# One decoder block kernel: head pairs issued in turn on TensorE, one score bank moved, search flags and the first residual rows reordered

## The chip, the cores and the metric

The kernel runs on one core of one Trainium2 chip, as one launch. The metric is the device time of a launch in microseconds (us). Three runs of the kernel before gave 3902.55, 3918.41 and 3919.11 us (median 3918.41). The profiled execution took 3900.74 us, of which its span is 3899.0 us.

## The reference

The input is x with 256 tokens of width 2048, float32. Two transformer blocks follow each other.

- Block one projects rms_norm(x) into four mixers: differential attention (4 heads, two 64-wide score maps a head), an RG-LRU, forgetting attention (4 heads of 128), and sliding-window attention with sinks (8 heads of 64, 2 key/value heads). Each is gated, the sum goes through w_out into the residual, and a SwiGLU feed-forward follows.
- Block two has dilated attention, NSA attention, cross attention to 256 memory rows, and a PEER layer.
- NSA has 16 query heads of 64 on 2 key/value heads. Each head attends in three branches: to 15 compressed keys, to the selected keys, and to a window. With 256 tokens the second and third use the same causal mask here. The three outputs are weighted by sigmoid gates and added.
- PEER has 8 heads. Each takes the 16 best of 128 by 128 expert pairs out of two sums of 128 scores, softmaxes them into gates, and all 16384 experts are computed densely: `gelu(v @ expert_u.T)` times the gate matrix, times `expert_v`.

What the change touches is, in the reference's words:

```python
logits = einsum('bqhmd,bshmd->bmhqs', q, k)     # differential, 2 maps of 64
logits = einsum('bnqkgd,bnskd->bnkgqs', q, k)   # sliding window, heads of 64
out    = einsum('bnkgqs,bnskd->bnqkgd', p, v)
# NSA: the same for compressed, selected and window keys, heads of 64
# PEER: top 16 of pair sums -> softmax -> dense gates; h += (gelu(x U) * gates) V
```

## The kernel before

Activations lie feature-major: 16 chunks of 128 features by 256 tokens. Every weight chunk is 1 MB (128 partitions by 2048 floats). SyncE's queue brings the chunks, in the order of `weight_stream`, into a ring of four. For float32 accuracy each chunk is split in two halves of 1024 columns. ScalarE writes the rounded part `wh` (L1130) and VectorE the remainder `wl` (L1768). Both hold four halves, so they can be at most two chunks ahead of TensorE. TensorE multiplies with three products: wh by x high and wh by x low (L519, L520), then wl by x high (L527). A chunk is one output tile (`tile_T`), 48 matmuls, and its result lies in PSUM bank 0 or 1 until ScalarE has evacuated it. A block of rows of a residual product (`rows`, L608, L610, L615) accumulates into all 8 banks instead.

No planner orders the work. Each engine's program is written out by hand, and they meet on counters: `full_a/full_v` says that a bank is ready for ScalarE or VectorE, `free_a/free_v` that it was read. `reserve(b)` lets TensorE wait for both free counters of a bank. `take(b)` is the reader's wait.

- **Pairs of heads.** Queries of two 64-wide heads (or two maps) lie in partitions 0 to 63 and 64 to 127 of one tile `qs`. The scores of a head are two float32 matmuls, for query block 0 against 128 keys and query block 1 against 256 (L682, helper `qk`). Differential and sliding-window attention call `qk` once per head. NSA calls it four times a pair, head by head and in a head branch by branch, into banks 2 to 5. A float32 matmul leaves two records in the trace.
- **Values.** `pv_T` (L701, L702) multiplies a head's probabilities for key block 0 (256 queries) and key block 1 (128 queries) with values of 64 columns. The heads of a pair write partitions 0 to 63 and 64 to 127 of bank 6. `nsa_values` does head 0 with two branches and its compressed product (L959, 15 rows), then head 1.
- **Order in an NSA pair.** Tile, transposed probabilities of the previous pair (L695, L948), tile, compressed scores into banks 6 and 7 (L975), scores, values of the previous pair, tile, tile (from pair 4 on a product `parts_T` in place of the last tile). VectorE reads the compressed scores at L2347, then the scores (L1859), takes the maximum, and normalises after ScalarE's exps. ScalarE evacuates the third tile's gate (L1514) only after its exps. From pair 4 on VectorE applies gates to banks 2 to 5 (L2387).
- **Search.** 128 expert tiles follow in PEER: 112 tiles, 64 rows of expert_v (`residual("v0")`), 16 tiles, 64 rows (`residual("v1")`). During the first 28 tiles VectorE also runs the top-16 searches, 8 parts a head. After every two heads it raises the flag `top_m` (L1753). ScalarE waits for it, does an Exp on `wts` (L1699) between its Gelus (L1703), and VectorE divides by the sum two tiles later and lets GpSimd scatter the gates. The tiles at which this happens are WEIGHT_TILES = (0, 8, 18, 28), and ScalarE waits at the tile at which VectorE raises the flag.
- **Last tile before a residual.** ScalarE rounds the first two activation rows into `xkh` (L1171). VectorE, in `last_rows`, does half a weight split, the two remainders `xkl` (L1779), and the other half. `rows` takes banks 0, 1, 2, 3 in order, two tiles each; bank 1 is still held by the last tile's Gelu.

Of the kernel before, what the change touches and what calls it, by code (L numbers as in the profile page):

```python
# [24 lines left out]
P = 128  # L25
D = 2048
T = 256
# [177 lines left out]
def build(nc, dram, out):  # L205
# [4 lines left out]
    with ctx:  # L210
# [192 lines left out]
        MEM_SQUARES = 12  # L403
        WEIGHT_TILES = (0, 8, 18, 28)
        block = ctx.enter_context(nc.Block())
# [47 lines left out]
        def _(pe):  # L453
# [140 lines left out]

            def rows(first, last):

                x = k.n["got xkl_ready"] % 2
                pe.wait_ge(*k.next("xkl_ready"))
                for t0 in range(0, KC, 8):
                    j = high()  # L600
                    for t in range(t0, t0 + 8):
                        o = ps[:, t // 2, (t % 2) * T:(t % 2 + 1) * T]
                        c = slice(t % 8 * P, (t % 8 + 1) * P)
                        if first and t % 2 == 0:
                            reserve(t // 2)
                        if first and t == 14:
                            wide(j, 7)
                        begin(mm(o, wh[:, j, c], xkh[:, x, :], start=first and t % 2 == 0, stop=False,  # L608
                                 skip_group_check=True), t % 8 == 0)
# [10 lines left out]
            def residual(name, n):  # L620

                rows(True, False)
# [53 lines left out]
            def qk(b, q, key, lo=0, hi=P, more=None, full=False):  # L676
# [8 lines left out]
                m.then_inc(*k.up(f"full_v{b}"))  # L685

            BLOCKS = ((0, 0), (1, 0), (1, 1), (0, 1))

# [10 lines left out]
            def pv_T(o, v, m, first, last):  # L699

                mm(o, v(0), pt[:, m, 0:T], start=first, stop=False, skip_group_check=True)  # L701
                return mm(o[:, P:T], v(1), pt[:, m, T:T + P], start=False, stop=last, skip_group_check=True)  # L702


# [34 lines left out]
            for h in range(4):  # L739
# [9 lines left out]
                staged(0)  # L749
                for m in range(2):  # L750
                    qk(2 + m, qs[:, 0], ks[:, 0], 64 * m, 64 * m + 64)
                fill_gate(4 * h + 1)
# [57 lines left out]
            for pair in range(4):  # L810
# [4 lines left out]
                staged(0)  # L815
                for hh in range(2):
                    qk(2 + hh, qs[:, 0], ks[:, 1 + pair // 2], 64 * hh, 64 * hh + 64)
                fill_gate(4 * pair + 1)
# [6 lines left out]
                g = pair // 2  # L825
                for hh in range(2):
                    m = pv_T(ps[64 * hh:64 * hh + 64, 6, 0:T], lambda kt: vs[:, 0, kt, 64 * g:64 * g + 64],
                             hh, True, True)
                m.then_inc(*k.up("full_v6"))
                fill_mix(2, pair, 2 if pair == 3 else None)  # L830
# [121 lines left out]
            def nsa_values(g):  # L952

                reserve(6)
                for hh in range(2):
                    o = ps[64 * hh:64 * hh + 64, 6, 0:T]
                    for br in range(2):
                        pv_T(o, lambda kt: vs[:, br, kt, 64 * g:64 * g + 64], 2 * hh + br, br == 0, False)
                    m = mm(o, vcd[0:C_CMP, g, :], ptc[0:C_CMP, hh, :], start=False, stop=True,  # L959
                           skip_group_check=True)  # L960
                m.then_inc(*k.up("full_v6"))

            for pair in range(8):
# [7 lines left out]
                staged(0)  # L971
                reserve(6, 7)
                for hh in range(2):
                    for i in range(2):
                        m = mm(ps[:, 6 + hh, i * 16:i * 16 + C_CMP], qs[64 * hh:64 * hh + 64, 0, i * P:(i + 1) * P],  # L975
                               kcd[64 * hh:64 * hh + 64, g, 0:C_CMP], start=True, stop=True)
                    m.then_inc(*k.up(f"full_v{6 + hh}"))
                for hh in range(2):
                    for br in range(2):
                        qk(2 + 2 * hh + br, qs[:, 0], kd[:, br, g], 64 * hh, 64 * hh + 64)  # L980
                if pair:
# [118 lines left out]
            residual("v1", HALF)  # L1100
            sum_squares()
# [3 lines left out]
        def _(act):  # L1105
# [607 lines left out]
            for c in range(HALF + AWAY):  # L1713
# [25 lines left out]
        def _(dve):  # L1739
# [603 lines left out]
            def nsa_scores(pair):  # L2343

                for hh in range(2):
                    take(6 + hh)
                    v.scalar_tensor_tensor(  # L2347
                        sc[:, hh, :, 0:C_CMP], nd_cmp[:], slope(2 * pair + hh + SLOPE_B),
                        ps[:, 6 + hh, 0:32].rearrange("p (i c) -> p i c", i=2)[:, :, 0:C_CMP],
                        ALU.mult, ALU.add).then_inc(*k.up(f"free_v{6 + hh}"))  # L2350
                for hh in range(2):
                    for br in range(2):
                        score(2 * hh + br, nd_causal[:], slope(2 * pair + hh + SLOPE_B))
# [268 lines left out]

            def weights_asked(turn):

# [26 lines left out]
            for c in range(16):  # L2651
# [3 lines left out]
                if c == 13:  # L2655
                    weights_asked(0)
# [12 lines left out]
            for c in range(HALF + AWAY):  # L2669
                last_rows(c, HALF + AWAY)  # L2670
                if c < 28:
                    searches(c + 12)
                if c in WEIGHT_TILES:
                    if c:
                        weights_asked(WEIGHT_TILES.index(c))
                elif c - 2 in WEIGHT_TILES:
                    weights_normed(WEIGHT_TILES.index(c - 2))
            residual(ag, "v0", HALF, early=True, group=gate_group)
# [227 lines left out]
```

## Time and profile before

| | us |
|---|---|
| runs shown | 3902.55, 3918.41, 3919.11 |
| profiled execution | 3900.74 |
| its span | 3899.0 |
| TensorE matmul busy | 3851.2 (99%) |
| VectorE busy | 2330.2 (60%) |
| ScalarE busy | 1885.3 (48%) |
| GpSimd busy | 569.5 (15%) |

The page's first part has busy time, share of the span and number of instructions of each engine. In a timeline a line has start, duration, engine, line of the kernel, output from input, the partitions by columns of the array's use, the shape of the moving operand, and the count of merged records. In square brackets stands idle time before it and what ended it. A float32 matmul's end is modelled, so distances between starts are what a stretch costs.

### The profile page before, as it was taken

What the parts mean: (1) busy time and instruction counts of PE and PEld (TensorE: products, weight loads), DVE (VectorE), ACT (ScalarE), POOL (GpSimd) and SP (SyncE); (2) the same over time, 40 slices, a digit from 0 to 9 for tenths busy, and PEclk for the clock granted to TensorE, in tenths of its full rate; (3) what the DMA queues carried; (4) which work ended last, traced back from release to release, by engine and by line L of the source; (5) the groups of instructions that cost most, each with busy time, mean ns of one, the idle gap of its engine ahead of it and who ended that gap; (6) DMA issues with size and microseconds to landing.
All of it is one profiled execution on the core that took longest, in us unless ns stands there. A gap on an engine that the chain in (4) does not pass through costs nothing.

```text
span 3899.0 us, 80514 instructions
## 1 busy us (share of the span) xinstructions
PE 3851.2 (99%) x33349; PEld 3811.6 (98%) x33349; DVE 2330.2 (60%) x3261; ACT 1885.3 (48%) x2592; POOL 569.5 (15%) x360
## 2 busy tenths in 40 slices
PE   8999999999999999999999999999999999999998
PEld 7999999999999999999999999999999999999998
DVE  7655565565555556554675766995444455555555
ACT  7555554454444444445654454444444444444443
POOL 2000000001000000000000000287888500000000
PEclk9999999999999999999999999999999999999999
DMA  5445455578555555544335544566677766676663
GB/s 215 182 166 183 175 184 184 195 270 280 193 194 194 194 192 182 182 173 146 136 132 194 178 168 152 173 185 204 193 215 217 226 221 215 221 259 213 215 220 134
DMA packets 161057, 755.81 MB, mean 194 GB/s; under 512 B 49376, under 2 KB 55648, under 8 KB 79040
## 3 DMA queue, kind: packets, MB, share of 16 engines
q1 hardware_dynamic: 105904, 701.55, 50.3%
q0 software_dynamic: 48016, 44.72, 5.4%
q10 hardware_dynamic: 6912, 6.29, 0.5%
q8 instruction: 171, 2.80, 0.3%
q14 instruction: 54, 0.44, 0.0%
HBM read 727.20 MB, written 25.30 MB: 193 GB/s over the span
## 4 chain that ended last, share of the span: by engine, by line
PE 91%; DVE 6%; ACT 1%; issue 1%; DMA 0%; DVEq 0%; SPq 0%; ACTq 0%
PE ps L519 18%; PE ps L527 18%; PE ps L520 18%; PE ps L608 10%; PE ps L615 10%; PE ps L610 10%; DVE wl L1768 2%; PE ps L575 1%; PE ps L576 1%; PE ps L580 1%; PE ps L682 1%; PE ps L701 1%; PE ps L695 1%; ACT wh L1130 1%; PE ps L637 0%
## 5 line engine op out<-in xcount | busy, mean ns | idle before, releaser
L1768 DVE TENSOR_TENSOR wl<-raw,wh 128x1024 fp32r<-128x1024 f32 x1328 | 1623.7, 1230 | 1378.6 <-ACT wh L1130 1373.5
L1130 ACT ACTIVATE wh<-raw 128x1024 fp32r<-128x1024 f32 x1328 | 1404.5, 1061 | 1854.2 <-PE ps L608 598.9
L519 PE MATMUL ps<-x,wh 128*128 128x256 f32 x6560 | 1548.5, 279 | 5.3 <-ACT ag L1703 3.4
L520 PE MATMUL ps<-x,wh 128*128 128x256 f32 x6560 | 1536.6, 277 | 0.0
L519 PEld LDWEIGHTS ps<-x,wh 128*128 128x128 f32 x6560 | 1235.0, 188 | 13.1 <-issue 6.1
L520 PEld LDWEIGHTS ps<-x,wh 128*128 128x128 f32 x6560 | 1235.0, 188 | 0.5
L527 PE MATMUL ps<-x,wl 128*128 128x256 f32 x6560 | 881.3, 277 | 0.3 <-DVE wl L1768 0.3
L527 PEld LDWEIGHTS ps<-x,wl 128*128 128x128 f32 x6560 | 808.2, 188 | 0.8 <-DVE wl L1768 0.8
L608 PE MATMUL ps<-xkh,wh 128*128 128x256 f32 x3328 | 776.6, 276 | 3.4 <-DVE xkl L1779 1.8
L610 PE MATMUL ps<-xkl,wh 128*128 128x256 f32 x3328 | 775.6, 276 | 0.0
L608 PEld LDWEIGHTS ps<-xkh,wh 128*128 128x128 f32 x3328 | 624.8, 188 | 5.2 <-DVE xkl L1779 2.8
L610 PEld LDWEIGHTS ps<-xkl,wh 128*128 128x128 f32 x3328 | 624.7, 188 | 0.0
L2785 POOL DMA_INDIRECT gates<-wts,gidx x256 | 474.1, 1852 | 330.8 <-DVE wts L2635 231.4
L615 PE MATMUL ps<-xkh,wl 128*128 128x256 f32 x3328 | 445.0, 276 | 0.0
L615 PEld LDWEIGHTS ps<-xkh,wl 128*128 128x128 f32 x3328 | 408.2, 188 | 0.0
L575 PE MATMUL ps<-y,wh 128*128 128x256 f32 x448 | 125.5, 280 | 0.0
L576 PE MATMUL ps<-y,wh 128*128 128x256 f32 x448 | 124.3, 277 | 0.0
L580 PE MATMUL ps<-y,wl 128*128 128x256 f32 x448 | 124.2, 277 | 0.0
L2799 POOL DMA_DIRECT2D gbuf<-gates x32 | 24.1, 755 | 669.1 <-DVE ag L2642 665.8
L2744 POOL MEMSET zeros<- 128x256 f32 x1 | 0.3, 313 | 755.6 <-DVE small L1753 755.6
L2767 POOL DMA_DIRECT2D small_w<-in_w_bgate x1 | 0.6, 592 | 587.3 <-DVE small L1753 587.3
L575 PEld LDWEIGHTS ps<-y,wh 128*128 128x128 f32 x448 | 84.6, 189 | 0.7 <-issue 0.7
(385 smaller groups left out, 2350.7 us busy)
## 6 DMA issues: line engine op xcount, KB each, us to landing
raw<-in_w_in SPq DMA_DIRECT2D x184, 1024.0 KB
raw<-in_expert_u SPq DMA_DIRECT2D x128, 1024.0 KB
raw<-in_expert_v SPq DMA_DIRECT2D x128, 1024.0 KB
raw<-in_w_ffn_gate SPq DMA_DIRECT2D x44, 1024.0 KB
raw<-in_w_ffn_up SPq DMA_DIRECT2D x44, 1024.0 KB
raw<-in_w_ffn_down SPq DMA_DIRECT2D x44, 1024.0 KB
raw<-in_w_out SPq DMA_DIRECT2D x32, 1024.0 KB
raw<-in_w_branch SPq DMA_DIRECT2D x16, 1024.0 KB
```

The costliest lines, as they stand in the source:

```text
L519: begin(mm(o, wh[:, j, c], x_h[:, kc, :], start=kc == 0, stop=False), kc % 8 == 0)
L520: mm(o, wh[:, j, c], x_l[:, kc, :], start=False, stop=False)
L527: m = mm(o, wl[:, j, c], x_h[:, kc, :], start=False, stop=kc == KC - 1)
L575: begin(mm(o, wh[:, j, c], yh[:, y0 + n, :], start=n == 0, stop=False), kc % 8 == 0)
L576: mm(o, wh[:, j, c], yl[:, y0 + n, :], start=False, stop=False)
L580: m = mm(o, wl[:, j, c], yh[:, y0 + n, :], start=False, stop=n == nk - 1)
L608: begin(mm(o, wh[:, j, c], xkh[:, x, :], start=first and t % 2 == 0, stop=False, skip_group_check=True), t % 8 == 0)
L610: mm(o, wh[:, j, c], xkl[:, x, :], start=False, stop=False, skip_group_check=True)
L615: m = mm(o, wl[:, j, c], xkh[:, x, :], start=False, stop=last, skip_group_check=True)
L1130: f(wh[:, u % 4, 0:width], raw[:, ring, c:c + width], ACT.Copy).then_inc(*k.up("hi"))
L1768: v.tensor_tensor(wl[:, u % 4, 0:width], raw[:, ring, c:c + width], wh[:, u % 4, 0:width].bitcast(F32), ALU.subtract).then_inc(*k.up("lo"))
L2785: g.indirect_dma_start(gates, bass.IndirectOffsetOnAxis(ap=gidx[:, h, i, s:s + 1], axis=0), wts[:, i, at_s:at_s + 1], None, compute_op=ALU ...
```

## The change

- `qk_two` issues the two heads' products in turn, query block by query block. Differential, sliding-window and NSA scores use it. NSA goes branch by branch. VectorE reads the scores in that order.
- `pv_two` issues the two heads' value products in turn, key block by key block. `nsa_values` does branch 0 of both heads, branch 1 of both, then both compressed products.
- The compressed scores lie in banks 0 and 7 in place of 6 and 7, also in turn.
- The search flag is raised at tiles 7, 17, 27 (was 8, 18, 28). ScalarE's Exp stands at tiles 0, 9, 19, 29 (was 0, 8, 18, 28). VectorE's division stands at tiles 1, 10, 20, 30 (was 2, 10, 20, 30).
- In the first block of rows of v0 and v1, bank 1's two tiles come last among the first eight. In the last tile before them VectorE does the two `xkl` before both halves of the split.

```diff
+        CMP_BANKS = (0, 7)
+        SEARCHED = (7, 17, 27)
...
-                    for t in range(t0, t0 + 8):
+                    for n, t in enumerate(sorted(range(t0, t0 + 8), key=lambda t: t // 2 == late)):
...
+            def qk_two(banks, q, key):
+                reserve(*banks)
+                for i in range(2):
+                    seen = T if i else P
+                    for hh, b in enumerate(banks):
+                        r = slice(64 * hh, 64 * hh + 64)
+                        m = mm(ps[:, b, i * T:i * T + seen], q[r, i * P:(i + 1) * P], key[r, 0:seen], start=True, stop=True)
+                        if i:
+                            m.then_inc(*k.up(f"full_v{b}"))
...
+            def pv_two(v, maps, first, last):
+                for kt in range(2):
+                    for hh in range(2):
+                        o = ps[64 * hh:64 * hh + 64, 6, kt * P:T]
+                        m = mm(o, v[:, kt, :], pt[:, maps[hh], kt * T:T + kt * P], start=first and kt == 0,
+                               stop=last and kt == 1, skip_group_check=True)
+                return m
...
             def nsa_values(g):
                 reserve(6)
+                for br in range(2):
+                    pv_two(vs[:, br, :, 64 * g:64 * g + 64], (br, 2 + br), br == 0, False)
                 for hh in range(2):
-                    o = ps[64 * hh:64 * hh + 64, 6, 0:T]
-                    for br in range(2):
-                        pv_T(o, lambda kt: vs[:, br, kt, 64 * g:64 * g + 64], 2 * hh + br, br == 0, False)
-                    m = mm(o, vcd[0:C_CMP, g, :], ptc[0:C_CMP, hh, :], start=False, stop=True,
-                           skip_group_check=True)
+                    m = mm(ps[64 * hh:64 * hh + 64, 6, 0:T], vcd[0:C_CMP, g, :], ptc[0:C_CMP, hh, :], start=False,
+                           stop=True, skip_group_check=True)
                 m.then_inc(*k.up("full_v6"))
...
-                for hh in range(2):
-                    for br in range(2):
-                        qk(2 + 2 * hh + br, qs[:, 0], kd[:, br, g], 64 * hh, 64 * hh + 64)
+                for br in range(2):
+                    qk_two((2 + br, 4 + br), qs[:, 0], kd[:, br, g])
...
-            residual("v0", HALF)
+            residual("v0", HALF, late=1)
...
-                if c in WEIGHT_TILES:
-                    weights(WEIGHT_TILES.index(c))
+                if c == 0:
+                    weights(0)
+                elif c - 2 in SEARCHED:
+                    weights(1 + SEARCHED.index(c - 2))
...
                 if c == n - 1:
-                    half()
                     early_rows(ag)
-                    half()
-                else:
-                    split()
+                split()
...
+                if c in SEARCHED:
+                    weights_asked()
+                elif c == 1:
+                    weights_normed(0)
+                elif c - 3 in SEARCHED:
+                    weights_normed(1 + SEARCHED.index(c - 3))
```

## Rows read from the trace of the kernel before

**Rows 1.** The page: busy time by engine, and the granted clock in 40 slices
```profile
PE 3851.2 (99%) x33349; PEld 3811.6 (98%) x33349; DVE 2330.2 (60%) x3261; ACT 1885.3 (48%) x2592; POOL 569.5 (15%) x360
PEclk9999999999999999999999999999999999999999
```

**Rows 2.** Timeline of TensorE, second NSA pair
```profile
1874.34 0.63 PE L975 MATMUL ps<-kcd,qs 64*128 64x15 f32 x8
1874.81 2.32 PE L682 MATMUL ps<-kd,qs 64*128 64x128 f32 x16
1877.05 0.65 PE L701 MATMUL ps<-pt,vs 128*64 128x256 f32 x2
1877.54 0.38 PE L702 MATMUL ps<-pt,vs 128*64 128x128 f32 x2
1877.76 0.59 PE L701 MATMUL ps<-pt,vs 128*64 128x256 f32 x2
1878.19 0.38 PE L702 MATMUL ps<-pt,vs 128*64 128x128 f32 x2
1878.50 0.64 PE L959 MATMUL ps<-ptc,vcd 15*64 15x256 f32 x2
1879.07 0.65 PE L701 MATMUL ps<-pt,vs 128*64 128x256 f32 x2
...
1881.08 0.39 PE L519 MATMUL ps<-x,wh 128*128 128x256 f32 x1
```

**Rows 3.** Timeline of TensorE, second sliding-window pair
```profile
511.45 0.93 PE L682 MATMUL ps<-ks,qs 64*128 64x128 f32 x8
512.31 0.38 PE L519 MATMUL ps<-x,wh 128*128 128x256 f32 x1
...
529.53 0.66 PE L701 MATMUL ps<-pt,vs 128*64 128x256 f32 x4
530.01 0.40 PE L702 MATMUL ps<-pt,vs 128*64 128x128 f32 x4
530.34 0.38 PE L575 MATMUL ps<-y,wh 128*128 128x256 f32 x1
```

**Rows 4.** Timeline of TensorE, the first NSA pair and the start of the third
```profile
1846.72 0.63 PE L975 MATMUL ps<-kcd,qs 64*128 64x15 f32 x8
...
1861.48 0.39 PE L519 MATMUL ps<-x,wh 128*128 128x256 f32 x1 [0.88 <-ACT mix L1514]
...
1892.09 0.28 PE L519 MATMUL ps<-x,wh 128*128 128x256 f32 x1
```

**Rows 5.** Timelines of VectorE and TensorE around banks that NSA frees
```profile
1876.68 0.40 DVE L2347 SCALAR_TENSOR_TENSOR sc<-nd_cmp,par,ps 128x30 f32<-128x30 f32 x2
...
2016.14 1.41 DVE L2387 TENSOR_TENSOR mix<-ps,mix 128x256 f32<-128x256 f32 x4
...
2019.48 1.48 PE L695 MATMUL ps<-ident,pr 128*128 128x128 f32 x12
```

**Rows 6.** Windows, expert tiles 2 to 9 and 10 to 32: busy us (records)
```profile
2489.21:2532.73 43.52, 43.52 (x386) 43.52 (x385) 41.30 (x116) 20.77 (x25) 24.54 (x14) 1.00 0.59 176
2532.73:2662.88 130.15, 126.67 (x1107) 125.69 (x1105) 116.50 (x336) 62.29 (x78) 106.37 (x59) 1.00 0.69 190
```

**Rows 7.** Timelines of ScalarE, VectorE and TensorE around the flag at tile 18
```profile
2591.78 0.26 ACT L1699 ACTIVATE wts<-wts 128x64 f32<-128x64 f32 x1 [6.91 <-DVE small L1753]
...
2593.09 1.23 DVE L1768 TENSOR_TENSOR wl<-raw,wh 128x1024 fp32r<-128x1024 f32 x1 [1.35 <-ACT wh L1130]
...
2595.68 0.38 PE L519 MATMUL ps<-x,wh 128*128 128x256 f32 x1 [2.31 <-ACT ag L1703]
```

**Rows 8.** Waits of TensorE's weight loads, 2480 to 2700 us
```profile
PEld ps L527 <- DVE wl L1768: 0.4, 2, 0.2
```

**Rows 9.** Timeline of TensorE, first rows of v0
```profile
3093.07 0.39 PE L608 MATMUL ps<-xkh,wh 128*128 128x256 f32 x1 [0.27 <-DVE xkl L1779]
...
3094.22 0.38 PE L608 MATMUL ps<-xkh,wh 128*128 128x256 f32 x1 [0.41 <-ACT gt L1703]
```

More of the change, by code:

```diff
@@ L403, in build @@
         MEM_SQUARES = 12
-        WEIGHT_TILES = (0, 8, 18, 28)
+        CMP_BANKS = (0, 7)
+        SEARCHED = (7, 17, 27)
         block = ctx.enter_context(nc.Block())
@@ L593, in fill_mix, with rows @@
                 marks["wb", n, q] = k.n[f"full_v{mix_banks(n, q)[-1]}"]
-            def rows(first, last):
+            def rows(first, last, late=None):
                 x = k.n["got xkl_ready"] % 2
@@ L608, in rows @@
                         begin(mm(o, wh[:, j, c], xkh[:, x, :], start=first and t % 2 == 0, stop=False,
-                                 skip_group_check=True), t % 8 == 0)
+                                 skip_group_check=True), n == 0)
                         mm(o, wh[:, j, c], xkl[:, x, :], start=False, stop=False, skip_group_check=True)
@@ L618, in rows, with residual @@
                             m.then_inc(*k.up(f"full_v{t // 2}"))
-            def residual(name, n):
-                rows(True, False)
+            def residual(name, n, late=None):
+                rows(True, False, late)
                 rows(False, False)
@@ L749, in _ @@
                 staged(0)
-                for m in range(2):
-                    qk(2 + m, qs[:, 0], ks[:, 0], 64 * m, 64 * m + 64)
+                qk_two((2, 3), qs[:, 0], ks[:, 0])
                 fill_gate(4 * h + 1)
@@ L815, in _ @@
                 staged(0)
-                for hh in range(2):
-                    qk(2 + hh, qs[:, 0], ks[:, 1 + pair // 2], 64 * hh, 64 * hh + 64)
+                qk_two((2, 3), qs[:, 0], ks[:, 1 + pair // 2])
                 fill_gate(4 * pair + 1)
@@ L825, in _ @@
                 g = pair // 2
[L826 to L829, printed above, removed]
+                pv_two(vs[:, 0, :, 64 * g:64 * g + 64], (0, 1), True, True).then_inc(*k.up("full_v6"))
                 fill_mix(2, pair, 2 if pair == 3 else None)
@@ L971, in _ @@
                 staged(0)
[L972 to L975, printed above, removed]
+                reserve(*CMP_BANKS)
+                for i in range(2):
+                    for hh, b in enumerate(CMP_BANKS):
+                        m = mm(ps[:, b, i * 16:i * 16 + C_CMP], qs[64 * hh:64 * hh + 64, 0, i * P:(i + 1) * P],
                                kcd[64 * hh:64 * hh + 64, g, 0:C_CMP], start=True, stop=True)
-                    m.then_inc(*k.up(f"full_v{6 + hh}"))
-                for hh in range(2):
-                    for br in range(2):
-                        qk(2 + 2 * hh + br, qs[:, 0], kd[:, br, g], 64 * hh, 64 * hh + 64)
+                        if i:
+                            m.then_inc(*k.up(f"full_v{b}"))
+                for br in range(2):
+                    qk_two((2 + br, 4 + br), qs[:, 0], kd[:, br, g])
                 if pair:
@@ L1096, in _ @@
                     keys_of(7)
-            residual("v0", HALF)
+            residual("v0", HALF, late=1)
             for c in range(HALF - AWAY):
                 tile_T(c % 2, spare=None if c else 7)
-            residual("v1", HALF)
+            residual("v1", HALF, late=1)
             sum_squares()
@@ L2343, in nsa_scores @@
             def nsa_scores(pair):
-                for hh in range(2):
-                    take(6 + hh)
+                for hh, b in enumerate(CMP_BANKS):
+                    take(b)
                     v.scalar_tensor_tensor(
                         sc[:, hh, :, 0:C_CMP], nd_cmp[:], slope(2 * pair + hh + SLOPE_B),
[L2349 to L2352, printed above, removed]
+                        ps[:, b, 0:32].rearrange("p (i c) -> p i c", i=2)[:, :, 0:C_CMP],
+                        ALU.mult, ALU.add).then_inc(*k.up(f"free_v{b}"))
+                for br in range(2):
+                    for hh in range(2):
                         score(2 * hh + br, nd_causal[:], slope(2 * pair + hh + SLOPE_B))
@@ L2621, in search, with weights_asked @@
                     step(v.tensor_copy(gidx[:, h], place))
-            def weights_asked(turn):
+            def weights_asked():
                 flag("top_m")
@@ L2655, in _ @@
                 if c == 13:
-                    weights_asked(0)
+                    weights_asked()
             def last_rows(c, n):
                 if c == n - 1:
-                    half()
                     early_rows(ag)
-                    half()
-                else:
-                    split()
+                split()
                 if c == n - 3:
@@ L2672, in _ @@
                     searches(c + 12)
[L2673 to L2677, printed above, removed]
+                if c in SEARCHED:
+                    weights_asked()
+                elif c == 1:
+                    weights_normed(0)
+                elif c - 3 in SEARCHED:
+                    weights_normed(1 + SEARCHED.index(c - 3))
             residual(ag, "v0", HALF, early=True, group=gate_group)
```

## The prediction

> **What bounds the kernel.** I read the page first. The reader is to see there that TensorE's matmuls are busy 99% of the span at the full granted clock, while VectorE is at 60% and ScalarE at 48% [rows 1]. So only what shortens TensorE's own stream, or one of its few waits, moves the end. I then followed TensorE's timeline through the stretches that the change touches, and read distances between starts, not durations. Last I looked at windows of VectorE, whose mean hides a stretch at 90 to 95% [rows 6].
>
> **Scores and values in NSA.** In the second NSA pair the scores' 8 products (16 records) take from 1874.81 to 1877.05, 2.24 us, and the values from 1877.05 to 1881.08, 4.03 us [rows 2]. A sliding-window pair shows what two heads cost when they run side by side. Its 4 score products (8 records) take 0.86 us from first start to the next tile, and the values of both heads (8 records) take 0.81 [rows 3]. One head's values for one branch take (1877.76 to 1878.19) 0.43 for the two 256-wide records and (1877.54 to 1877.76) 0.22 for the two 128-wide, so 0.65 [rows 2]. Two heads in the sliding window cost 0.81 with the edges. They overlap almost wholly, and they do so in the kernel before, where they are issued head after head. So issue order alone is not what decides. It is distance: in NSA the second head's values come after ten records of the first head with a change of array shape in between, and there nothing overlaps.
>
> - *NSA scores.* After: the first branch of both heads costs what the sliding window's does, 0.86, and the second adds the streaming of one head's branch, 0.65. That is 1.51 in place of 2.24, 0.73 less. The bounds are nothing (the reordering that the engine does by itself stays as it is, 2.24) and 2.24 less twice 0.65, 0.94. I take 0.73, as both its parts are rows of the same shapes.
> - *NSA values.* Each head's part is (1877.05 to 1879.07) 2.02 us: two branches and the 15-row product [rows 2]. Side by side the second head's 2.02 vanish, as it does in rows 3. The upper bound is just that 2.02, the lower the two changes of shape alone. These changes show as 1878.19 to 1878.50 in place of 0.22, and 1878.50 to 1879.07 in place of 0.43, so 0.09 and 0.14, 0.23 together. I take 2.0.
> - *How many.* Values are done 8 times. Scores are done 8 times, but in the first pair there are no values yet, and TensorE waits there already: it starts the next pair's tile at 1861.48, when ScalarE has evacuated the gate of bank 0 [rows 4]. What the scores save there goes into that wait. So 7 x 0.73 + 8 x 2.0 = 5.1 + 16.0 = 21.1 us.
> - *Is something late next?* The ScalarE chain of rows 4 lets the next pair start 1861.48 - 1846.72 = 14.76 us after the compressed scores' start. In the second pair TensorE starts 1892.09 - 1874.34 = 17.75 after it, and would after the change start 17.75 - 2.73 = 15.02 after it. 0.26 is left, so the chain stays just hidden. From pair 4 on VectorE's four gate products of banks 2 to 5 start at 2016.14, 0.35 each, and the transposes that need the banks one after another start at 2019.48, after the change at 2016.75, at 12 records in (1.31 us) 0.33 a bank [rows 5]. Bank 2 is free at 2016.5, bank 5 at 2017.55 and wanted at 2016.75 + 0.98 = 2017.73. Again hidden, by 0.2 us. If either cover were gone by x us, 7 (or 3) times x is lost.
>
> **Compressed scores in banks 0 and 7.** VectorE reads them at 1876.68 for 0.40 us, two reads [rows 5]. It can't do so earlier, since it has a weight half to finish. Before, TensorE reached the values at 1877.05 and the wait for bank 6 cost nothing. After, it reaches them at 1876.3, and with bank 6 it would wait about 0.7 us a pair. With bank 0 the wait moves to the next tile, at 1877.05 - 0.73 + 2.0 = 1878.3, 1.2 us after VectorE is done. Queued behind it are only that tile and what follows. So the move gains nothing by itself and keeps 0.7 x 7 = 5 us of the sum. The alternation of the eight short records has no room: they already take 0.47 us [rows 2].
>
> **Differential and sliding-window scores and values.** 8 score pairs and 4 value pairs are reordered. They take 0.86 and 0.81 already [rows 3]. The stream of one head alone is 0.65, so at most 0.2 could go and that is the edge. I take 0 (bounds 0 and 12 x 0.1).
>
> The Trainium skill (TensorE: Matmul & The Clock Gate, "The mechanism") says that matmuls start and end in strict program order and only weight loads are pulled ahead. By it two heads issued one after the other overlap only where they meet, and these 12 places would gain, as an estimate, 0.4 us each, 5 us more. The trace disagrees: 8 score records of 0.65 us a head end within 0.86.
>
> The Trainium skill (TensorEngine Tiling (Array Packing), "Key Properties") says that a change of tiling mode drains the array. The trace agrees, with the 0.09 and 0.14 us above.
>
> **Search flags.** Tiles 2 to 9 take 43.52 us, 5.44 each. Tiles 10 to 32, 23 of them, take 130.15 in place of 125.12: 5.03 us are lost [rows 6]. The largest piece is at the flag of tile 18: ScalarE waits 6.91 us for VectorE's flag, can't evacuate the next tile's bank, and TensorE stands 2.31 us [rows 7]. After the change the flag is raised one tile earlier by VectorE and wanted one tile later by ScalarE, two tiles (10.9 us) against a wait of 6.91, so it goes. The Exp and its table loads stay. What is late next is VectorE: it is busy 116.5 of 130.15 us here [rows 6], and its remaining idle time is mostly its own wait for ScalarE at the flags, 1.35 us [rows 7], at three flags. That idle time goes too, so VectorE gets up to 1.35 us earlier per flag, while TensorE gets earlier by 2.5. At tiles 20 and 30 the weight remainders were already late by 0.4 us in all [rows 8], and before the third flag VectorE has gained 2 x 1.35 = 2.7 against TensorE's 2.7 to 3.0. So about 0.5 us of remainder waits stay. Gain 5.03 - 0.5 = 4.5 us, with bounds 5.0 (none stay) and 1.5 (TensorE runs up against VectorE and only what VectorE gains, less a tile's slack, is left). GpSimd's scatters may start one tile earlier for the first two heads. Nothing waits for them until v0, so 0.
>
> **First rows.** TensorE starts v0's rows late, by 3093.07 less the 3092.64 at which it was due (0.11 after its last matmul), 0.43, for `xkl`. After four matmuls it stands again until the Gelu has freed bank 1, 3094.22 [rows 9]. After the change `xkl` is done before the last tile's halves, in time in which VectorE was idle. TensorE starts at 3092.64, does 12 matmuls at 0.113 before it needs bank 1, and is there at 3094.0, 0.2 early. Bank 1 is free as before. It then has 4 matmuls left of the 16 in place of 12, so it gains 8 x 0.113 = 0.9 us. For v0 and v1: 1.8 us. The bounds are 0 (VectorE's halves, now behind `xkl`, come late) and 2.0.
>
> **Sum.** 21.1 + 0 + 4.5 + 1.8 = 27.4 us. The profiled execution would take 3900.74 - 27.4 = 3873.3. It lies at the lower end of the runs shown (3902.55), while the median is 3918.41 and two runs are near it. I take the sum off the median: 3891.0 us.
>
> **Rivals.**
> 1. *A hidden chain surfaces in NSA.* The covers are 0.26 and 0.2 us. If ScalarE's exps or VectorE's products come 1 us later to TensorE's clock, since TensorE no longer gives them the time, 7 us go: 20 us left, 3898. For: the covers are thin. Against: both chains start from the end of the tile before the scores, which doesn't move against them. Chance 0.12.
> 2. *VectorE sets the pace in the search.* Only 1 of the 4.5 us comes: 3894.5. For: 90% busy. Chance 0.10.
> 3. *Values don't overlap in NSA.* Accumulating two branches in one bank with alternating halves could order them. Then 8 x 0.23 in place of 16.0 is gained from values, 14.2 less: 13.2 us in all, 3905. For: nothing overlapped there before. Against: the sliding window writes the same two halves of the same bank side by side [rows 3]. Chance 0.09.
> 4. *Slower: taking turns costs a drain each time.* If each step between heads made the array wait as a change of shape does (0.09 and 0.14 us, and a first weight load uncovered), and the side-by-side running of today were lost, the scores of sliding window and differential would go from 0.86 to 2 x 0.65 + 3 x 0.15 = 1.75 (8 times, +7), their values the same (4 times, +4), the NSA scores to 4 x 0.65 + 7 x 0.15 = 3.65 (8 times, +11), the compressed scores +0.5 (8 times, +4), and the NSA values by 8 x 0.15 = 1.2 (8 times, +10). 36 less 6.3 for search and rows: 30 us slower, 3948. It decides once the turns cost more than the 6.3 us, about 0.04 a turn over 150 turns. For: the change alternates at every product. Against: 8 score records in 0.86 us leave room for no drain between heads [rows 3]. Chance 0.03.
>
> **How the numbers follow.** The forecast has 0.66. Its own range is 3868 to 3896: the bounds of the parts (24 to 30 us) off either cluster of runs. Rivals 1 to 3 stretch the upper end to 3906. The range 3868 to 3906 leaves out rival 4 and some drift. A measurement tells 0.5%, about 19.6 us, from no change. The forecast, rivals 1 and 2 (barely) lie beyond it, rival 3 within. With what the two clusters of runs may blur: faster 0.77, same 0.20, slower 0.03.
>
> **What would show it.** In the profile after: the NSA pair's period falls from 30.6 (1861.48 to 1892.09 [rows 4]) to about 27.8 us, with L682's 16 records within 1.5 us and the values within 2.1. The differential and sliding-window stretches stay at 0.86 and 0.81. ScalarE's wait at L1699 is gone, and TensorE shows under 1 us of waits for L1703 and L1768 in the search, with the 23 tiles in 125.6 us. `rows` starts 0.11 us after the last tile. The prediction is wrong if TensorE waits for L1514 or L2387 in pairs 1 to 7, or if the values keep 4 us.

## The result, and the profile after

Over eight runs each the changed kernel took 3880.61 us in the median (3872.26 to 3892.36) and the kernel before 3901.54 (3899.35 to 3919.11). The ratio is 0.9934 with a 95% interval of 0.9914 to 0.9955. So the changed kernel is faster, by 0.66%, but the interval reaches from 0.45% to 0.86%.

Both medians hide that the runs fall into two clusters, 18 us apart. Before, five runs took 3899.35 to 3902.55 us and three 3918.41 to 3919.11. After, four took 3872.26 to 3874.00 and four 3887.21 to 3892.36. No run lies near 3880.61, which is the middle of the gap. From the median of the lower cluster to that of the lower cluster the gain is 28.1 us (3900.45 to 3872.35), and so it is from upper to upper (3918.48 to 3890.42). The profiled execution lies in the lower cluster, as the one before does. It took 3872.26 us with a span of 3870.5, against 3900.74 and 3899.0: 28.5 us less.

In six of the twelve experiments below, the stretch of the expert tiles took 17 to 18 us longer for a reason that none of their edits has (last section). So what a part costs is read from the stretch that the edit changes, and the table at the head of the experiments says where the rest of each span went.

The page after has nearly the same busy shares, and its clock row has a 9 in all 40 slices, as before. This is its engine row.

```profile
PE 3828.3 (99%) x33349; PEld 3797.5 (98%) x33349; DVE 2329.4 (60%) x3261; ACT 1885.4 (49%) x2592; POOL 574.4 (15%) x360
```

**NSA.** The timeline of TensorE in the second NSA pair of the changed kernel; it answers to [rows 2]. Columns are start, duration, engine, line, operands, shapes and merged records.

```profile
1873.45 1.56 PE L695 MATMUL ps<-kd,qs 64*128 64x128 f32 x16
1874.94 1.52 PE L721 MATMUL ps<-pt,vs 128*64 128x256 f32 x16
...
1876.97 0.39 PE L520 MATMUL ps<-x,wh 128*128 128x256 f32 x1
...
1887.97 0.28 PE L520 MATMUL ps<-x,wh 128*128 128x256 f32 x1
```

The scores take 1873.45 to 1874.94, 1.49 us in place of 2.24. The values take 1874.94 to 1876.97, 2.03 in place of 4.03. The pair's period (1860.12 below to 1887.97) is 27.85 us, against 30.61 [rows 4].

The first pair and the start of the second, in the same timeline:

```profile
1845.36 0.62 PE L990 MATMUL ps<-kcd,qs 64*128 64x15 f32 x8
1845.83 1.56 PE L695 MATMUL ps<-kd,qs 64*128 64x128 f32 x16
1847.99 0.38 PE L520 MATMUL ps<-x,wh 128*128 128x256 f32 x1 [0.60 <-DVE sc L2364]
...
1860.12 0.38 PE L520 MATMUL ps<-x,wh 128*128 128x256 f32 x1 [0.56 <-ACT mix L1529]
```

Here the new use of bank 0 makes a wait. With no values between scores and tile, the tile stands 0.60 us until VectorE has read the bank. It costs nothing: 1860.12 - 1845.36 = 14.76 us, exactly as before, set by ScalarE's gate.

**First block.** The timeline of the sliding-window stretch of [rows 3] after the change:

```profile
511.41 0.93 PE L695 MATMUL ps<-ks,qs 64*128 64x128 f32 x8
512.26 0.39 PE L520 MATMUL ps<-x,wh 128*128 128x256 f32 x1
...
529.48 0.87 PE L721 MATMUL ps<-pt,vs 128*64 128x256 f32 x8
530.28 0.38 PE L576 MATMUL ps<-y,wh 128*128 128x256 f32 x1
```

Scores 0.85 us, values 0.80: as before.

**Search.** The window of the same tiles 10 to 32 as in [rows 6]; tiles 2 to 9 take 43.52 us as before. After the window's bounds stands its length, then busy time and records of PE, PEld, DVE, ACT and POOL, the granted clock, and two figures on DMA.

```profile
2510.08:2636.22 126.14, 125.67 (x1106) 125.28 (x1105) 116.54 (x335) 63.85 (x78) 103.04 (x55) 1.00 0.70 197
```

The 23 tiles take 126.14 us in place of 130.15. The wait at `wts` is gone (timeline of ScalarE around tile 19), and TensorE's weight loads now wait for VectorE's remainders (their waits, 2440 to 2700 us).

```profile
2566.03 1.28 ACT L1714 ACT_TABLE_LOAD   x1
2567.32 0.26 ACT L1714 ACTIVATE wts<-wts 128x64 f32<-128x64 f32 x1
```
```profile
PEld ps L528 <- DVE wl L1785: 0.9, 2, 0.5
```

**First rows.** The timeline of TensorE at v0's first rows, answering to [rows 9]:

```profile
3065.98 0.28 PE L609 MATMUL ps<-xkh,wh 128*128 128x256 f32 x1
...
3067.23 0.28 PE L611 MATMUL ps<-xkl,wh 128*128 128x256 f32 x1
3067.56 0.39 PE L609 MATMUL ps<-xkh,wh 128*128 128x256 f32 x1
```

It starts at once, and what is left of bank 1's wait is the step from 3067.23 to 3067.56, 0.22 us more than the usual 0.11 from one matmul to the next.

The difference of the profiled executions by stretch, from the starts of the same matmuls in both:

| stretch | before | after | gained |
|---|---|---|---|
| start to the first NSA pair's third tile | 1849.44 | 1847.99 | 1.45 |
| NSA and up-projections, to 2100.85 / 2078.26 | 251.41 | 230.27 | 21.14 |
| to expert tile 2 | 388.36 | 388.30 | 0.06 |
| expert tiles 2 to 32 | 173.67 | 169.66 | 4.01 |
| first rows of v0 and v1 | | | 1.83 |

Together 28.49 of 28.5 us. The 1.45 us can't be put down to the change. They come in the main from the stretch between the last values of the dilated attention and the first compressed scores, where both kernels have the same program. Its windows, before and after:

```profile
1782.85:1846.72 63.87, 63.87 (x511) 63.32 (x510) 26.58 (x32) 27.42 (x41) 0.00 (x0) 0.92 0.36 126
```
```profile
1783.08:1845.36 62.28, 62.28 (x512) 61.73 (x510) 26.58 (x32) 27.41 (x41) 0.00 (x0) 0.95 0.37 130
```

The mean granted clock is 0.92 in the one and 0.95 in the other, and the stretch is 1.59 us shorter. In experiments 1 and 12 the clock is 1.00 there and it takes 59.24 us. Over the fourteen profiled executions it takes 59.24 to 64.02 us.

### The profile page after: what moved, and what is told of

Same layout as the page of the kernel before. It is cut to its first block, busy times and chain, and to the rows that moved or that the text cites. A ratio compares the mean times of both kernels' runs of the same rounds, so it can differ in the third digit from the quotient of the medians.

```text
span 3870.5 us, 80544 instructions
## 1 busy us (share of the span) xinstructions
PE 3828.3 (99%) x33349; PEld 3797.5 (98%) x33349; DVE 2329.4 (60%) x3261; ACT 1885.4 (49%) x2592; POOL 574.4 (15%) x360
## 4 chain that ended last, share of the span: by engine, by line
PE 92%; DVE 6%; ACT 1%; issue 1%; DMA 0%; DVEq 0%; SPq 0%; ACTq 0%
PE ps L520 18%; PE ps L528 18%; PE ps L521 18%; PE ps L616 10%; PE ps L609 10%; PE ps L611 10%; DVE wl L1785 2%; PE ps L576 1%; PE ps L577 1%; PE ps L581 1%; PE ps L707 1%; ACT wh L1145 0%; PE ps L695 0%; PE ps L721 0%; PE ps L683 0%
```

## The experiments

All start from the changed kernel and undo or alter one thing. The two kernels themselves and the forecast name the theory: distance in the instruction stream decides whether two heads overlap, and each other part removes one stall. The rivals stand in each expectation.

Each experiment but the last is a single run. The table has its span less the changed kernel's 3870.5 us, and where that lies: ahead of the NSA pairs, from the first compressed scores to the first expert Gelu, from there to v0's rows, and behind.

| | expected | measured | ahead | NSA | expert tiles | behind |
|---|---|---|---|---|---|---|
| 1 | 16.0 | 35.6 | -3.3 | 20.8 | 17.9 | 0.1 |
| 2 | 5.2 | 5.8 | 0.0 | 5.7 | 0.1 | 0.1 |
| 3 | 0 | 21.5 | 2.7 | 1.3 | 17.4 | 0.0 |
| 4 | 5.3 | 11.6 | 1.0 | 10.5 | 0.0 | 0.1 |
| 5 | 0 to 0.8 | 20.5 | 1.7 | 0.8 | 18.0 | 0.0 |
| 6 | 0.1 | 3.7 | 3.1 | 0.5 | 0.0 | 0.1 |
| 7 | 4.6 | 5.8 | -0.4 | 6.2 | 0.0 | 0.0 |
| 8 | 4.0 | 22.6 | 0.6 | 0.7 | 21.3 | 0.0 |
| 9 | -0.7 | -0.2 | 0.0 | 0.8 | -1.0 | 0.0 |
| 10 | 1.8 | 20.5 | -0.4 | 1.1 | 18.0 | 1.8 |
| 11 | 0.5 | 19.5 | 0.1 | 1.1 | 18.3 | 0.0 |
| 12 | -1.6 | -3.8 | -3.0 | 0.1 | -1.0 | 0.0 |

So no span alone confirms an expectation. What is ahead of NSA is in good part the granted clock, as above. NSA differs by up to 1.1 us between executions whose program is the same there (6, 8, 9, 10, 11).

**1. Values put back**, each head's compressed product behind its own branches.

```diff
-                for br in range(2):
-                    pv_two(vs[:, br, :, 64 * g:64 * g + 64], (br, 2 + br), br == 0, False)
+                for hh in range(2):
+                    for br in range(2):
+                        pv_T(o, ..., 2 * hh + br, br == 0, False)
...
```

> The changed kernel with the NSA values alone put back (head 0 with both branches and its compressed product, then head 1). Theory, distance decides: the second head comes ten records after the first with a change of shape between, so the values take 4.03 us a pair again in place of 2.03, 8 x 2.0 = 16.0 us more, span 3886.5. The scores stay at 1.49 us. Rival, the values are only faster because they no longer stand behind unpaired scores: then they stay near 2.0 and the span at 3870.5.

The values take 1871.69 to 1875.72, 4.03 us, in its timeline:

```profile
1870.20 1.56 PE L695 MATMUL ps<-kd,qs 64*128 64x128 f32 x16
1871.69 0.65 PE L713 MATMUL ps<-pt,vs 128*64 128x256 f32 x2
...
1875.72 0.38 PE L520 MATMUL ps<-x,wh 128*128 128x256 f32 x1
```

The values of all eight pairs take 2.0 us more (7 x 2.00 and 1.97), 16.0 in all, as the theory has it. The scores stay at 1.49.

NSA as a whole lost 20.8 us and not 16.0. From pair to pair it takes 30.35 us where 27.73 and 2.00 would make 29.73. The missing 0.6 lies in the tiles behind the values, up to the transposes: the matmuls there come 118 ns apart in place of 113, at a granted clock of 1.00 and with GpSimd idle (129 in 15 us, 134 in the changed kernel).

```profile
1876.00:1891.00 15.00, 15.00 (x129) 15.00 (x129) 11.70 (x19) 10.47 (x26) 0.00 (x0) 1.00 0.11 31
```

The kernel before has the same values and 113 ns there, so this is not the price of the order. The last section comes back to it.

**2. Values head by head, but the compressed products behind both.** Eight records of one head, then eight of the other, without a change of shape between.

```diff
-                for br in range(2):
-                    pv_two(vs[:, br, :, 64 * g:64 * g + 64], (br, 2 + br), br == 0, False)
+                for hh in range(2):
+                    for br in range(2):
+                        pv_T(ps[64 * hh:64 * hh + 64, 6, 0:T], ..., 2 * hh + br, br == 0, False)
```

> The changed kernel with the NSA values head by head (8 records of head 0, then 8 of head 1), the two compressed products behind both. Theory, distance decides and 8 is too far for the whole of it, as in the scores of the kernel before (head 0's first branch alone, the middle side by side, head 1's last alone): 0.65 us alone at each end, so 1.45 + 0.65 = 2.1 for the branches in place of 1.45, 5.2 us more, span 3875.7. Rival, only the change of shape between the heads kept them apart: 0 more.

Its timeline:

```profile
1874.96 0.65 PE L713 MATMUL ps<-pt,vs 128*64 128x256 f32 x2
1875.44 0.38 PE L714 MATMUL ps<-pt,vs 128*64 128x128 f32 x2
1875.66 0.65 PE L713 MATMUL ps<-pt,vs 128*64 128x256 f32 x4
1876.09 0.44 PE L714 MATMUL ps<-pt,vs 128*64 128x128 f32 x4
1876.37 0.59 PE L713 MATMUL ps<-pt,vs 128*64 128x256 f32 x2
1876.80 0.38 PE L714 MATMUL ps<-pt,vs 128*64 128x128 f32 x2
1877.11 0.65 PE L976 MATMUL ps<-ptc,vcd 15*64 15x256 f32 x4
```

The counts are to be read: x2, then x4, then x2. In the order of the program that can only be head 0's first branch alone, its second side by side with head 1's first, and head 1's second alone. 2.15 us in place of 1.45, 0.70 a pair, 5.6 in all (5.2 expected). So of the 2.0 us a pair, 0.70 came from distance alone, and the other 1.3 from the 15-row product that stood between the heads. Whether it is that product's shape or its two further records wasn't separated: no run has a product of full shape there.

**3. Values branch by branch, in a branch head after head.** Four records apart in place of two.

```diff
+                for br in range(2):
+                    for hh in range(2):
+                        pv_T(ps[64 * hh:64 * hh + 64, 6, 0:T], ..., 2 * hh + br, br == 0, False)
```

> The changed kernel with the NSA values branch by branch, but inside a branch head 0's two products and then head 1's (4 records apart in place of 2). Theory, the engine itself pulls the other head's product ahead over a distance of 4 records, as in the sliding window: values stay at 2.03 us, span 3870.5. Rival, only taking turns product by product overlaps both: each branch then overlaps only where the heads meet, 0.2 to 0.4 us more a branch, 3 to 6 us more in all.

```profile
1878.05 0.66 PE L713 MATMUL ps<-pt,vs 128*64 128x256 f32 x4
...
1878.75 0.65 PE L713 MATMUL ps<-pt,vs 128*64 128x256 f32 x4
...
1879.55 0.65 PE L976 MATMUL ps<-ptc,vcd 15*64 15x256 f32 x4
```

The branches' records come four at a time; 1878.05 to 1879.55 is 1.50 us against 1.45. The engine overlaps over four records by itself. Taking turns product by product is worth 0.05 us a pair, the order of the branches the rest.

**4. Scores put back, and 5. scores branch by branch, head after head** (the two loops below exchanged).

```diff
-                for br in range(2):
-                    qk_two((2 + br, 4 + br), qs[:, 0], kd[:, br, g])
+                for hh in range(2):
+                    for br in range(2):
+                        qk(2 + 2 * hh + br, qs[:, 0], kd[:, br, g], 64 * hh, 64 * hh + 64)
```

> The changed kernel with the NSA scores alone put back (head 0 branch 0, head 0 branch 1, head 1 branch 0, head 1 branch 1). Theory: the scores take 2.24 us again in place of 1.49, in 7 pairs 0.75 each, 5.3 us more, span 3875.8; the first pair loses nothing, since ScalarE's gate of bank 0 holds the next tile there. Rival, the compressed scores' bank gives the gain: then 0 more.

> The changed kernel with the NSA scores branch by branch, but inside a branch head 0's two products and then head 1's (4 records apart). Theory: 1.49 to 1.6 us, up to 0.1 more in 7 pairs, span 3870.5 to 3871.3. Rival, taking turns by product is what pays: 1.49 becomes about 1.9, 2.9 us more.

Timelines of the one and of the other:

```profile
1874.48 2.32 PE L683 MATMUL ps<-kd,qs 64*128 64x128 f32 x16
1876.72 1.52 PE L721 MATMUL ps<-pt,vs 128*64 128x256 f32 x16
```
```profile
1875.20 1.66 PE L683 MATMUL ps<-kd,qs 64*128 64x128 f32 x16
1876.79 1.52 PE L721 MATMUL ps<-pt,vs 128*64 128x256 f32 x16
```

The scores take 2.25 us and 1.59 us, against 1.49. The first pair loses nothing in either. Of 0.76 us a pair, 0.66 is the order of the branches and 0.10 the turns. The same picture as with the values, now for row halves in place of column halves of the array. NSA as a whole lost 10.5 us in experiment 4, twice what was expected. Every second pair takes 29.31 us in place of the 28.49 that 0.76 more makes, again with matmuls 118 ns apart behind the values; the rest was lost behind the last pair.

**6. First block put back**: scores of the dilated attention and of the sliding window, and the values of both, head after head.

```diff
-                qk_two((2, 3), qs[:, 0], ks[:, 0])
+                for m in range(2):
+                    qk(2 + m, qs[:, 0], ks[:, 0], 64 * m, 64 * m + 64)
...
```

> The changed kernel with the differential and sliding-window scores and values of the first block put back, head after head. Theory: the engine overlapped them already, 0.863 in place of 0.856 us for scores (8 places) and 0.808 in place of 0.801 for values (4 places), 0.08 us more in all. Rival, by strict program order: 0.4 us more at each of 12 places, 5 us.

```profile
512.00 0.93 PE L683 MATMUL ps<-ks,qs 64*128 64x128 f32 x8
512.86 0.38 PE L520 MATMUL ps<-x,wh 128*128 128x256 f32 x1
```

All eight scores take 0.86 us, and all four values 0.81 where the changed kernel has 0.80. The rival's 0.4 us occurs at none of the twelve places. These edits do nothing.

**7. Compressed scores in banks 6 and 7.**

```diff
-        CMP_BANKS = (0, 7)
+        CMP_BANKS = (6, 7)
```

> The changed kernel with the compressed scores back in banks 6 and 7. Theory: TensorE reaches the values 1.96 us after the compressed scores' start, and VectorE has read bank 6 about 2.6 us after it, so TensorE waits 0.65 us in each of 7 pairs, 4.6 us more, span 3875.1. The 0.66 us that the first pair waits for bank 0 in the changed kernel goes but gains nothing. Rival, the move is free either way: span 3870.5 (it cost nothing in the kernel before, where TensorE came 0.7 us later).

```profile
1873.05 1.56 PE L695 MATMUL ps<-kd,qs 64*128 64x128 f32 x16
1875.21 1.52 PE L721 MATMUL ps<-pt,vs 128*64 128x256 f32 x16 [0.60 <-DVE sc L2364]
```

The values start 2.16 us after the scores in place of 1.49: 0.67 in each of seven pairs, 4.7 us. The move, worth nothing to the kernel before, holds 4.7 us of what the other edits gain.

**8. Old search flags**: Exp in the flagged tile itself, division two tiles later.

```diff
-        SEARCHED = (7, 17, 27)
+        SEARCHED = (8, 18, 28)
...
```

> The changed kernel with the search flags, Exps and divisions back at tiles 8, 18, 28 (and 0, 2). Theory: the three stalls of 0.22, 2.47 and 1.28 us and 0.35 us of restarts come back and the 0.7 us of waits for weight remainders shrink to 0.4, so 4.0 us more, span 3874.5. Rival, VectorE alone sets the pace and the stall only moved: under 1.5 us more.

Tiles 10 to 32, and the waits in the search:

```profile
2511.37:2641.93 130.56, 128.17 (x1107) 127.47 (x1105) 116.54 (x336) 62.29 (x78) 107.50 (x59) 0.99 0.70 190
```
```profile
ACT wts L1714 <- DVE small L1770: 15.5, 3, 6.9
PEld ps L520 <- ACT ag L1718: 2.8, 2, 2.5
PEld ps L528 <- DVE wl L1785: 0.2, 1, 0.2
```

The window takes 4.4 us more, near the 4.0 expected, but by luck, for it is made up otherwise. Two of the three stalls came back, 2.8 us together; the third, 1.28 us, did not. Behind the long one, in which TensorE had stood for 2.31 us, the granted clock fell to half, the lower of TensorE's two levels (1.2 and 2.4 GHz). It stayed there for 3.2 us, 15 matmuls at 0.21 us in place of 0.11, which cost 1.5 us:

```profile
2574.50:2577.90 3.40, 3.40 (x17) 3.40 (x18) 3.22 (x24) 1.93 (x3) 2.79 (x3) 0.51 0.72 236
```

In the kernel before the same stall left the clock at 1.00. In the window's last 11 us the matmuls are 118 ns apart, 0.4 us more. The remainder waits fall from 0.9 to 0.2 as TensorE is held back: part of what the flags gave is taken back by VectorE.

**9. Searches spread over 44 tiles.**

```diff
-            SLOTS = 40
+            SLOTS = 44
...
-            SEARCHED = (7, 17, 27)
+            SEARCHED = (9, 20, 31)
```

> The changed kernel with the same search parts spread over 44 tiles in place of 40, flags at tiles 9, 20, 31. Theory, VectorE's load causes the last 0.7 us of waits for weight remainders: they go, 0.7 us less, expert tiles 2 to 32 then take 5.44 us each. Rival, they stem from the Exps and table loads of ScalarE: they stay at 0.7.

```profile
2510.85:2635.97 125.12, 125.12 (x1106) 125.12 (x1105) 117.61 (x333) 60.93 (x75) 98.36 (x56) 1.00 0.69 195
```

The 23 tiles take 125.12 us, 5.44 each: nothing is lost any more, 1.0 us gained (0.7 expected). The last waits were VectorE's load, not ScalarE's Exps and table loads, which are all still there.

**10. Banks in order, and 11. `xkl` between the halves.**

```diff
-            residual("v0", HALF, late=1)
+            residual("v0", HALF)
```
```diff
                 if c == n - 1:
+                    half()
                     early_rows(ag)
-                split()
+                    half()
+                else:
+                    split()
```

> The changed kernel with banks 0, 1, 2, 3 in order in the first rows of v0 and v1. Theory: TensorE starts each at once but after 4 matmuls stands until the last Gelu has freed bank 1, 1.5 us after the start in place of 0.45: 0.9 us more per residual (8 matmuls less are placed before that wait), 1.8 us in all. Rival, the wait for xkl was the only one that counted: 0.9 us or less in all.

> The changed kernel with VectorE's two xkl of the last tile between the halves again. Theory: TensorE starts 0.43 us late, then runs its 12 matmuls and comes to bank 1 at a time when it is free, so 0.43 less the 0.2 that it waits there in the changed kernel, 0.2 to 0.3 us more per residual, 0.5 in all. Rival, the two parts add up by themselves: 0.43 each, 0.9 in all.

First rows of v1, in the tenth and in the eleventh:

```profile
3521.78 0.28 PE L611 MATMUL ps<-xkl,wh 128*128 128x256 f32 x1
3523.02 0.39 PE L609 MATMUL ps<-xkh,wh 128*128 128x256 f32 x1 [0.97 <-ACT ag L1718]
```
```profile
3521.62 0.39 PE L609 MATMUL ps<-xkh,wh 128*128 128x256 f32 x1 [0.27 <-DVE xkl L1796]
...
3522.99 0.28 PE L611 MATMUL ps<-xkl,wh 128*128 128x256 f32 x1
```

From the start of the first block to the next eight columns it is 3.97 us in the tenth, 3.06 in the changed kernel: 0.91 more, twice. In the eleventh the start of v1 is 0.43 late and the block 0.22 shorter, 0.21 more; that of v0 is 0.33 late, 0.11 more. Together that is 0.3 us, not 0.5. So the two edits aren't additive. Both stalls stood before the same Gelu: the earlier `xkl` alone brings nothing (the tenth, which has it, loses as much as the kernel before, whose start is 0.43 late and whose block takes 3.54), the bank order alone 0.7 to 0.8, both together 0.91.

**12. Full rows and spread searches.** With experiment 9's edit, and the compressed value product over all 128 rows (rows 15 to 127 are zero), so that the array needn't change its shape.

```diff
-  m = mm(..., vcd[0:C_CMP, g, :], ptc[0:C_CMP, hh, :], start=False,
+  m = mm(..., vcd[:, g, :], ptc[:, hh, :], start=False,
...
-  f(flat(ptc[0:C_CMP, :, :]), ps[0:C_CMP, 7, :], ACT.Copy)
+  f(flat(ptc[:]), ps[:, 7, :], ACT.Copy)
...
+  step(v.memset(vcd[:], 0.0))
```

> The changed kernel with the searches over 44 tiles, and the compressed value products over 128 rows in place of 15 (rows 15 to 127 are zero), so that the array keeps its shape through the values. Theory: the two changes of shape go, 0.578 us becomes about 0.44, 0.14 x 8 = 1.1 us less, of which in three pairs up to 0.1 comes back as waits for banks 2 to 5; with the searches 1.6 us less than the changed kernel in all. Rival, the cost is the weight load of a new product, not the shape: 0.7 less, from the searches alone.

```profile
1872.00 1.52 PE L721 MATMUL ps<-pt,vs 128*64 128x256 f32 x16
1873.35 0.60 PE L974 MATMUL ps<-ptc,vcd 128*64 128x256 f32 x4
1873.88 0.38 PE L520 MATMUL ps<-x,wh 128*128 128x256 f32 x1
```

The values take 1.88 us in place of 2.03, so the shape has a price and the rival falls. But the pairs don't keep the 0.145 us. From pair to pair it takes 27.62 us in place of 27.73 in the second to fourth, and 27.75 as in the changed kernel in the fifth to seventh. 27.62 is also what the first pair takes in nearly every execution, the kernel before included, where ScalarE's gate sets it; and from pair 5 on the transposes start later behind the tile by what was saved. The covers are used up. By period 0.4 us is left, and with at most 0.3 from the last two values and 1.0 from the searches it is 1.4 to 1.7 us, as expected. Over six runs the median is 3872.91 us (3868.43 to 3873.32), ratio to the kernel before 0.9921 (0.9900 to 0.9942). Its profiled span, 3866.7, is the lowest of all, but 3.0 of the 3.8 us are the granted clock ahead of NSA, 1.00 where the changed kernel has 0.95. The two intervals overlap, so a lead over the changed kernel (0.9934) isn't shown by the medians. What stands out is that none of its six runs lies in an upper cluster (last section).

## Why the prediction was right

- **NSA, 21.1 us forecast, 21.14 measured.** Scores 1.51 us a pair were forecast, 1.49 came; values 2.0 less, 2.00 came (experiments 1 and 4). That the sums agree to 0.04 us is chance, as the stretch itself differs by 1.1 us between like executions. The first pair's gain was absorbed by ScalarE's gate, as forecast. The step "distance, with a change of shape in between" was right but not split: experiment 2 shows 0.70 us of a pair's 2.0 to be distance, and 1.3 the product in between.
- **The two thin covers held, just.** The gate of bank 0 never made TensorE wait after the first pair, and a pair takes 27.73 us against the 27.62 of the first, which the gate bounds. The banks 2 to 5 did make it wait by a trace: the transposes of pairs 5 to 7 take 1.68 to 1.69 us in place of 1.67.
- **Banks 0 and 7: 0.7 us a pair forecast, 0.67 measured** (experiment 7). What the forecast left out is that the wait surfaces in the first pair, 0.60 us, hidden only by the later one.
- **First block: nothing forecast, nothing came** (experiment 6). The rule of the Trainium skill (TensorE: Matmul & The Clock Gate, "The mechanism") that matmuls never pass each other would have given 5 us. Experiment 3's counts of four show two heads side by side that are issued head after head.
- **Search: 4.5 us forecast, 4.01 measured.** The stalls went. The mis-sized term is what VectorE takes back: 0.5 us of remainder waits were forecast, 0.9 came, and 1.0 us with the restarts behind them. Before they were 0.4 [rows 8], in experiment 8 they are 0.2: VectorE catches up while TensorE stands, by more than the forecast took. Experiment 9 removes them by giving VectorE more tiles.
- **First rows: 1.8 us forecast, 1.83 measured**, with the 0.2 us left at bank 1.
- **The level was luck.** The sum of 27.4 us stands against 28.1 from cluster to cluster and 28.5 in the profiles, of which 1.45 belong to a stretch whose clock differs. So the mechanism and its size are right. The time, 3891.0, was taken off a median of three runs, 3918.41, that happened to lie in the upper cluster. It meets the upper cluster after (3890.42), and off the lower one the sum gives 3873.1, where 3872.35 came. Over eight runs the median before fell into the lower cluster and the one after into the gap. The forecast has no account of the clusters, only a range wide enough for both.

The rivals are decided. Values overlap (against 3), turns cost no drain (against 4: alternating is 0.05 to 0.10 us cheaper a pair than not), the hidden chains stayed hidden (against 1), and VectorE took back 1.0 us of the search and not 4.0 (against 2).

## What to carry to other kernels

Before interleaving small products by hand, look at the counts of merged records: where four come at a time the engine already runs two array halves side by side, and only products further apart, or with another product between, have anything to gain. A shortened stretch brings the next reader's buffer onto the path, so move its bank in the same edit, and price that move with the others in place: alone it looked worthless, and it held 4.7 us. Two stalls in front of one event don't add up; measure the pair. Where single runs fall into clusters, compare cluster with cluster, and look for the stretch that tells them apart before a span is held against a forecast.

## What the runs showed of the hardware

**Reach of the overlap.** With four records of the other array half ahead the engine pulls a product forward (experiments 3, 5 and 6). With eight ahead it does so only for the last four (experiments 2 and 4). With ten, and a 15-row product between, not at all (experiment 1). It holds for row halves writing different banks and for column halves writing one bank.

**Matmul spacing has two levels, at the same granted clock.** In experiment 3 TensorE makes 1700 matmuls from 2700 to 2900 us, in the changed kernel 1767:

```profile
2700.00:2900.00 200.00, 200.00 (x1700) 200.00 (x1700) 86.19 (x71) 84.74 (x106) 162.82 (x103) 1.00 0.70 195
```
```profile
2700.00:2900.00 200.00, 200.00 (x1767) 200.00 (x1766) 91.09 (x74) 87.64 (x111) 167.52 (x92) 1.00 0.74 206
```

The clock is 1.00 in both. The mean distance is 117.8 ns against 113.3. In six executions (experiments 1, 3, 5, 8, 10, 11) it stays at 117.8 for 460 to 500 us. The level begins at 2594 to 2631 us, in each of the six where TensorE restarts after a short wait in the search, with 53 or more of GpSimd's 256 indirect transfers already issued, and it ends 1 to 6 us after v0's rows begin.

GpSimd's scatter, first start to last, takes 516 to 525 us in these six and 562 to 574 in the other eight. It gets faster where the matmuls get slower, but it is not what holds them there. The last transfer starts 86 to 94 us before the level ends; in experiment 10 GpSimd does nothing from 3000 to 3075 us, and the 640 matmuls are still 117 to 118 ns apart:

```profile
3000.00:3075.00 75.00, 75.00 (x640) 75.00 (x639) 32.23 (x27) 32.42 (x41) 0.00 (x0) 1.00 0.63 218
```

The same level also shows for some 16 us at a time in the NSA pairs of experiments 1 and 4, with GpSimd idle, from a pair's values to its transposes. What chooses the level wasn't tried. The long stretch is worth 17 to 18 us, which is the distance of the two clusters; that the timed runs of the upper clusters have it is likely, but only profiled executions show it.

Of the twelve profiled executions with such a wait in the search six took the level up for long and six didn't. The two without any wait there, experiments 9 and 12, didn't, and the six timed runs of 12 all took 3868.43 to 3873.32 us, where four of the changed kernel's eight lie in the upper cluster. If the restart is what lets the level in, spreading the searches is worth far more than its 1.0 us. With seven executions that is a hint and not shown.
